# The end of an mLSTM layer: when the context rows are scaled and the latent tiles are gated

## The reference

```python
def finish(hsum, o, z):
    hh = jnp.moveaxis(hsum, 1, 2)                       # forward plus backward scan
    hh = hh * jax.nn.sigmoid(o)                         # gated
    hh = rmsnorm(hh, g_head)                            # squared, averaged per head, scaled
    return (hh * jax.nn.silu(z)) @ w_out                # scaled by z, projected

y_l = finish(hl_f + flip(hl_b), o_l, z_l)
y_c = finish(hc_f + flip(hc_b), o_c, z_c)
# per layer: x = x + gate * rmsnorm(y, g_post); gate, shift, scale come from silu(c) @ w_ada
```

## Time and profile before

| | |
|---|---|
| median of three runs | 1547.73 us (1542.19 to 1548.88) |
| the profiled execution | 1546.94 us, of which the span of the core is 1545.1 us |
| TensorE busy | 1458.6 us, 94% of the span |
| VectorE, ScalarE, GpSimd busy | 993.1, 754.6 and 67.6 us |
| mean granted TensorE clock | 0.988 of full speed |

### The profile page before, as it was taken

The page is one execution under the profiler, slowest core; times in us unless marked ns, Lnnn a source line. Parts: engine busy times, 40 slices in busy tenths (PEclk is TensorE's granted clock), DMA queues, the critical chain, the costliest instruction groups (busy, mean ns, idle before and its releaser), DMA issues.

```text
span 1545.1 us, 24102 instructions
## 1 busy us (share of the span) xinstructions
PE 1458.6 (94%) x9392; PEld 1195.3 (77%) x9392; DVE 993.1 (64%) x2286; ACT 754.6 (49%) x1630; POOL 67.6 (4%) x76
## 2 busy tenths in 40 slices
PE   6999999999999999999988999998899899899999
PEld 4777766777778777888767777676787798799987
DVE  3647677564667548545585668767767476777763
ACT  4445566453655443241233546655666347555542
POOL 0000000110000100020000100001101020000000
PEclk9999999999999999999999999999999999999999
DMA  9132270322640322222451145333535642445553
GB/s 364 58 109 83 98 270 2 102 83 69 254 170 1 109 89 83 94 82 82 181 188 55 56 164 153 109 105 120 178 129 145 208 150 96 160 155 188 185 188 136
DMA packets 59226, 202.84 MB, mean 131 GB/s; under 512 B 7054, under 2 KB 10344, under 8 KB 58984
## 3 DMA queue, kind: packets, MB, share of 16 engines
q1 hardware_dynamic: 52928, 192.84, 35.9%
q10 hardware_dynamic: 6008, 7.40, 2.1%
q0 software_dynamic: 176, 1.06, 0.2%
HBM read 199.43 MB, written 1.84 MB: 130 GB/s over the span
## 4 chain that ended last, share of the span: by engine, by line
PE 70%; DVE 17%; ACT 5%; issue 3%; DMA 3%; POOL 2%; ACTq 0%; SPq 0%; DVEq 0%; POOLq 0%
PE ps L2269 65%; PE ps L2272 5%; DVE w_l L2939 3%; DVE st L3038 2%; ACT w_h L2582 1%; DVE l_P L2943 1%; DVE x L2947 1%; ACT l_P L2585 1%; DMA w_l_ada<-in_l_ada 1%; DVE m_P L3522 1%; DMA w_raw<-in_l_out 1%; DVE l_xn L2943 1%; DVE l_h_lat L2947 1%; POOL mstat L3616 1%; DVE m_kn L2939 1%
## 5 line engine op out<-in xcount | busy, mean ns | idle before, releaser
L2939 DVE TENSOR_TENSOR w_l<-w_raw,w_h 128x1024 fp32r<-128x1024 f32 (+3 forms) x263 | 315.6, 1206 | 75.9 <-ACT w_h L2582 75.2
L2582 ACT ACTIVATE w_h<-w_raw 128x1024 fp32r<-128x1024 f32 (+3 forms) x263 | 272.7, 1044 | 102.9 <-DMA w_raw<-in_f_down 23.2
L2269 PE MATMUL ps<-w_h,l_hTh 128*128 128x512 f32 (+1 forms) x384 | 155.4, 405 | 0.5 <-DVE w_l L2939 0.4
L2269 PE MATMUL ps<-w_h,l_hTl 128*128 128x512 f32 (+1 forms) x384 | 151.1, 394 | 0.0
L2269 PE MATMUL ps<-w_l,l_hTh 128*128 128x512 f32 (+1 forms) x384 | 151.0, 393 | 0.0
L2585 ACT ACTIVATE l_P<-ps,st 128x512 f32<-128x512 f32 (+1 forms) x128 | 77.7, 609 | 88.0 <-DVE st L2947 60.4
L2269 PE MATMUL ps<-f_hTh,w_h 128*128 128x256 f32 x352 | 99.0, 281 | 0.0
L2269 PE MATMUL ps<-l_hTh,w_h 128*128 128x512 f32 (+1 forms) x264 | 98.4, 373 | 0.5 <-issue 0.5
L2269 PE MATMUL ps<-f_hTl,w_h 128*128 128x256 f32 x352 | 98.8, 281 | 0.0
L2269 PE MATMUL ps<-f_hTh,w_l 128*128 128x256 f32 x352 | 98.8, 281 | 0.0
L2269 PE MATMUL ps<-l_hTh,w_l 128*128 128x512 f32 (+1 forms) x264 | 97.7, 370 | 0.0
(11 more groups left out here) (446 smaller groups left out, 3449.2 us busy)
## 6 DMA issues: line engine op xcount, KB each, us to landing
w_two<-in_l_ada SPq DMA_DIRECT2D x24, 1024.0 KB, 6.8
w_raw<-in_l_z SPq DMA_DIRECT2D x32, 512.0 KB, 3.5
w_two<-in_l_adg SPq DMA_DIRECT2D x16, 1024.0 KB, 5.0
w_raw<-in_l_out SPq DMA_DIRECT2D x32, 512.0 KB, 3.5
w_raw<-in_m_merge SPq DMA_DIRECT2D x24, 512.0 KB, 3.4
w_raw<-in_f_gate SPq DMA_DIRECT2D x22, 512.0 KB, 3.2
w_raw<-in_f_up SPq DMA_DIRECT2D x22, 512.0 KB, 3.3
w_raw<-in_f_down SPq DMA_DIRECT2D x22, 512.0 KB, 3.2
```

Of the source, the lines that this page charges most:

```text
L2269: return p.e.matmul(out, lhsT, rhs, start=start, stop=stop)
L2582: return p.e.activation(out, a, func, scale=scale)
L2939: return p.e.tensor_tensor(out, a, b, op)
```

## The change

`Mlstm.finish` is cut in two: `rows_of(pair)` (gate, square, mean, scale) and `turned(pair, ...)` (transpose, affine, split).

- For the context, `chain` of both is the same order as before, but six pieces of it instead of three are emitted beside the first six pieces of `steps` in `layer_mlstm`: up to and with the scaling of both tiles.
- For the latent tiles, `rows_of((1,))` is braided with what is left of `steps` after three more pieces, that is with step 7, and `rows_of((0,))` comes behind it, all of it beside `mod` and `ctx`. In `turn` only `turned(LAT)` is left, eight pieces; two pieces of the out-projection are emitted first, and the eight are woven with its next six.

No arithmetic is added or taken away.

```diff
@@ turn
         if beside:
-            weave(beside, upto(half, 8), 8, 14)
+            drain(upto(half, 2))
+            weave(beside, upto(half, 6), 6, 8)
@@ layer_mlstm
-        gate, ctx = Gate(p, 2, *gate, f), m.finish(CTX, f, (2,))
+        gate, ctx = Gate(p, 2, *gate, f), chain(m.rows_of(CTX), m.turned(CTX, f, (2,)))
         mod = p.ada(PAIR, [(3, 0), (2, "gate"), (3, 1)], gate)
-        drain(braid(upto(steps, 6), upto(mod, 6), upto(ctx, 3)))
+        drain(braid(upto(steps, 6), upto(mod, 6), upto(ctx, 6)))
         gate.free = p.fence()
-        drain(braid(steps, mod, ctx))
+
+        def tail():
+            yield from upto(steps, 3)
+            yield from braid(steps, m.rows_of((1,)))
+            yield from m.rows_of((0,))
+        drain(braid(tail(), mod, ctx))
         p.W.split_to(len(p.W.order) + 1, len(p.W.order) + 1)
         f = p.fence()
-        lat = m.finish(LAT, f, TRANS)
+        lat = m.turned(LAT, f, TRANS)
@@ Mlstm
-    def finish(self, pair, fence, pool):
+    def rows_of(self, pair):
         p = self.p
-        hf_tok = [None, None]
         for t in pair:
             p.fin_o(self, t, [self.htok[t, h] for h in range(4)])
             yield
         ...
         for t in pair:
             p.fin_rows(self, t)
             yield
+
+    def turned(self, pair, fence, pool):
+        p = self.p
+        hf_tok = [None, None]
         for kp in range(4):
             ...
```

## The result

Over 22 runs each the changed kernel takes 1548.88 us (1545.16 to 1552.46) and the kernel before 1545.93 us (1542.19 to 1551.19): ratio 1.0018, 95% interval 1.0010 to 1.0026. So it is 2.9 us slower by the medians, within 0.5% and outside the runs' uncertainty. Two later measurements, of the same kernel and of one that differs by a single 0.1 us instruction, gave 1.0031 (1.0019 to 1.0044) and 1.0018 (1.0009 to 1.0027).

What follows compares the result with a forecast made beforehand. TensorE, busy for 94% of the span, bounds the kernel, with VectorE the limit from 797.0 to 817.2 us; 0.4 for order plus 1.2 and 0.4 for clock gives +2.0 on 1546.94, so 1548.9 us, range 1543 to 1555.

Steps and rivals of the forecast that it cites:

- Copies of step 6's denominator: VectorE's four copies, behind 3.25 us of context scalings, start at 785.35 instead of 782.43 us.
- The wait of 2.5 us: TensorE, ready for step 6's carry at about 783.15, waits 2.5 us for VectorE's copies, done at 785.65.
- Wait for the affine copy: Second context transposes ahead of step 7 wait 1.76 us for ScalarE's copy that empties their bank, until 792.5.
- Carry of step 7 done: TensorE finishes step 7's carry at 797.6 us instead of 795.19, so +2.4 us.
- Third block: Out-projection's third block waits for its weight rest on VectorE, done at 818.6 us; its matmuls started at 811.63 before.
- Net of the order against the profile of before: Out-projection's second tile: 823.55 against 823.45 us, with handovers +0.4 us, before any clock terms.
- The clock behind the wait ahead of step 6's carry: TensorE's low clock after 2.5 us idle slows step 6's carry by 1.8 us; two thirds taken, +1.2 us.
- The clock around the third block: Low clock may recur at the out-projection's third block, at most 0.8 us, and as much the block before; +0.4 taken.
- The signs of being wrong: First latent matmul before 826, step 6's carry without a wait, or a difference arising beyond 829 where no instruction moved.
- No term of the clock: Rival: TensorE waits but keeps its high level, step 6's carry stays 1.78 us; 1547.4 us, chance 0.2.
- Waits won: Rival: TensorE's waits for latent rows and a rest go, 4.7 us and some 2 of clock; around 1541, chance 0.15.
- Low clock through step 7: Rival: clock stays low from the first wait until step 7, +8 us; 1556 us, chance 0.1.

Runs made afterwards that it cites:

- inert edit: Kernel before with a GpSimd constant written in two halves, one 0.1 us instruction more: ratio 1.0001; the same edit in the changed kernel: 1.0018 against the kernel before.

## Why the prediction was right, and which step of it was not

Forecast 1548.9, measured 1548.88. The order of events was read rightly, the clock was not, and that the totals agree so closely is luck: the forecast put +2.0 us on a profiled execution of 1546.94, while over 22 runs the kernel before has a median of 1545.93 and the change adds 2.9. A starting point 1.0 too high and a difference 0.9 too small cancel. Step by step, positions from the stage transposes, where the prediction's zero is 779.02:

- *Copies of step 6's denominator*: predicted at 6.33 (785.35), they stand at 786.41 - 780.17 = 6.24. The wait of 2.5 us came as 0.95 + 1.27 = 2.22, in two pieces: six of the eight local products of step 6 wait for `l_C`, for in the kernel they take banks that the state of step 5 reads, and this state now stands behind the scalings of tile 2. That link was overlooked.
- *Wait for the affine copy*: 1.76 predicted, 1.15 measured. The copy of the gate row starts while TensorE is still in the last block, not when the blocks are done.
- *Carry of step 7 done*: +2.4 predicted, 18.18 - 16.17 = +2.0. The 16.17 of before has a slow carry in it; against 14.49 it is +3.7.
- *End of VectorE's additions*: 23.8 predicted (802.8), 803.35 + 0.17 - 780.17 = 23.35.
- *Waits of VectorE*: 1.0, 1.0 and 0.8 predicted; 1.12, 1.12 and 0.82.
- *Third block*: 39.6 predicted (818.6), 39.90.
- *Second tile's second block*: 44.9 predicted with the handovers; 825.14 - 780.17 = 44.97.
- *Net of the order against the profile of before*: +0.4 predicted, 49.67 - 49.12 = +0.55.
- *The clock behind the wait ahead of step 6's carry*: +1.2 taken. This is the step that failed. In all eight profiles with the early context rows this carry follows waits of 0.95 and 1.27 us and takes 1.99 us. The 1.13 us wait ahead of step 7's carry, on which the term rested, is followed by the low level in both profiles of the kernel before, and in none of the four others that have it. The rule of the Trainium skill, "TensorE: Matmul & The Clock Gate", "Why this matters for your kernels", which has longer gaps bring the clock down, fits these twelve profiles and not the other two; the prediction gave it 0.2.
- *The clock around the third block*: +0.4 taken. The low clock fell on the first block and cost nothing, as the third waits for its rest.
- *The signs of being wrong*: one was a difference that arises beyond 829. One did in the profile, 1.8 us in the changed kernel's favour, but the other two profiles with the same order take 718.5 and 716.8 us there, where the first has 715.2, and the other one of the kernel before 716.7. Profiles of one order differ there by more than 1.8 us, so it isn't the change's.

What the prediction missed is that its yardstick had a term of the same kind in it. The profile of before has 6.8 us of low clock on the way, and some 3.9 us of that reach the end: 1.7 at the carry and 2.3 behind it. The inert edit's profile has 2.6 of them less. Against the first yardstick the new order was to cost 0.4 and costs 0.55; against the second it costs 3.1, and with no low clock some 4.5 (estimate). So the +1.2 and +0.4 taken for the clock came near the measured difference for another reason than the one given. That this reason is the slowed baseline is argued, not shown. *No term of the clock*, the rival at 1547.4, describes the way in the profile better than the forecast does, and its time is 1.5 us below the median; from the median of before it would be 1546.4, 2.5 below. *Waits won* fell: no wait was won, they came back as others. *Low clock through step 7* fell: in the first profile the low clock comes only at 809 us, behind step 7.

The cause of the loss is shown as far as this: each part alone makes it; filling most of VectorE's three waits takes 2.0 us of the way and the loss in the median away. These two don't quite fit: at 47.62 the way is still some 2.4 us longer than that of before without low clock (45.2, estimate), and no run shows why the median is even. That VectorE's 3.64 us of idle time in step 7 is the context part's share is read from the trace, not isolated: no run gave the affine copy a second bank. Why the clock falls in one program at 611 us and in another at 791 us stays open, and so does whether executions without a profile have it at the same places.

## What to carry to other kernels

Where one engine's list sets the end, moving work up in it wins only if the place it goes to has a wait to fill; put there, it can open waits (a bank that isn't free, a copy in another engine's queue) that idle this very engine. A large wait of TensorE was worth nothing here while VectorE's list set what came next: 3.1 us taken away at one place came back at the next. Ask early for what another engine must answer (mean, then power), and put unrelated work between question and use.

Before a term of the clock goes into a sum, take it out of the baseline as well, or measure the baseline again with an edit that moves nothing. Here 2.6 us of a stretch of 49 went with an edit that moves nothing, and the low clock left in it was still 1.3. Of each low stretch ask whether a wait hides it.

## What the runs showed of the hardware

- The low clock comes in stretches that cost 1.7 us, or twice or three times that, when TensorE is busy: nine to thirteen such amounts in each of the 14 profiles, 15.4 to 22.2 us in all (span times what the mean clock lacks to 1). The three profiles with the change's order (one with the inert edit) have 17.1, 18.8 and 20.5 us of it and spans of 1545.0, 1546.3 and 1547.4.
- Where it falls depends on more than the waits beside it: the same instructions with the same wait of 1.13 us ahead had a slow carry in two profiles and not in four. Whether the additional 0.1 us GpSimd instruction at 0.7 us moved it, or the chip or the execution did, is open. Sixteen tiny matmuls (64x4, 1.94 us together) stand ahead of 611 us in every kernel; the clock fell behind them in 11 of 14 profiles.
- GpSimd's power on 128x4 took 1.01 us beside small work of VectorE, 1.18 beside scalings, and 1.91 beside a weight rest of 1024 columns. The Trainium skill, "Advanced Engine Details and Errata", "GPSIMD Details", has GpSimd share a read and a write interface with VectorE, in conflict with its instructions on two SBUF inputs: the rest is one of these, and the trace agrees. The scalings read two such inputs as well and lengthened the power only from 1.01 to 1.18, so it agrees in kind, and no run shows what sets the size.
